# A blocked RWKV inverse spread over all four 64x64 parts of TensorE, with another order on ScalarE, VectorE and GpSimd

## What is computed

```python
x = x + 0.5 * swiglu(rmsnorm(x, g), w_gate, w_up, w_down)       # every ffn stage
# the even stage, for 8 heads of width 64
def step(S, inp):
    Sa = einsum('bhvk,bhk->bhv', S, a_t)
    S = S * w_t + Sa[..., None] * b_t + v_t[..., None] * k_t
    return S, einsum('bhvk,bhk->bhv', S, r_t)
y = concat([y_conv, group_norm(scan(step)) * g]) @ w_out
```

## Time and profile before

| what | us |
|---|---|
| median of 3 runs | 1596.88 |
| lowest and highest of them | 1595.38, 1597.02 |
| the profiled execution, its own time | 1597.77 |
| its span | 1596.0 |
| its TensorE busy | 1543.1 |
| mean granted TensorE clock | 0.991 of full speed |

### The profile page before, as it was taken

How to read it: one execution, slowest core, us unless ns; L and a number is a source line. 1 busy time by engine, 2 the same in 40 slices (tenths; PEclk the granted TensorE clock), 3 DMA queues, 4 the chain that set the end, 5 groups by cost and what they waited for, 6 DMA issues and landing times.

```text
span 1596.0 us, 29271 instructions
## 1 busy us (share of the span) xinstructions
PE 1543.1 (97%) x11720; PEld 1419.5 (89%) x11720; DVE 790.1 (50%) x1053; ACT 766.6 (48%) x1054; POOL 515.2 (32%) x201
## 2 busy tenths in 40 slices
PE   7999999999999999999989999999999999999997
PEld 7999988887999998999976899999999987899996
DVE  4444446467544444434555544345443488754343
ACT  5444364335534453443565544436444478454433
POOL 2443400000444345344342243443434300043442
PEclk9999999999999999999999999999999999999999
DMA  6555431134545535544532355444554452245442
GB/s 254 200 190 197 171 119 68 55 108 158 192 169 192 196 120 198 195 178 178 201 115 74 124 198 192 181 179 163 196 197 183 172 198 93 91 174 197 175 180 92
DMA packets 48086, 259.93 MB, mean 163 GB/s; under 512 B 5376, under 2 KB 5632, under 8 KB 27296
## 3 DMA queue, kind: packets, MB, share of 16 engines
q1 hardware_dynamic: 47664, 258.68, 44.0%
q10 hardware_dynamic: 288, 0.34, 0.1%
q0 software_dynamic: 80, 0.14, 0.0%
HBM read 258.08 MB, written 1.05 MB: 162 GB/s over the span
## 4 chain that ended last, share of the span: by engine, by line
PE 89%; ACT 4%; DVE 4%; issue 1%; DMA 1%; POOL 1%; SPq 0%; DVEq 0%; POOLq 0%; ACTq 0%
PE banks L367 81%; PE banks L1257 1%; ACT gu_hi L338 1%; DVE gu_lo L347 1%; DMA raw_gu<-units_gu 1%; DVE x L474 1%; PE banks L1264 1%; ACT arena L402 1%; PE banks L2048 1%; PE banks L2643 0%; ACT h_hi L385 0%; PE banks L1234 0%; PE banks L2047 0%; DVE arena L2371 0%; ACT arena L2253 0%
## 5 line engine op out<-in xcount | busy, mean ns | idle before, releaser
L360 POOL TENSOR_TENSOR dn_lo<-raw_dn,dn_hi 128x1024 fp32r<-128x1024 f32 x138 | 479.9, 3477 | 905.9 <-ACT dn_hi L343 887.3
L367 PE MATMUL banks<-h_hi,gu_hi 128*128 128x256 f32 x2256 | 644.2, 286 | 11.3 <-DVE h_lo L418 6.7
L367 PE MATMUL banks<-h_hi,gu_lo 128*128 128x256 f32 x2256 | 640.3, 284 | 0.0
L367 PE MATMUL banks<-h_lo,gu_hi 128*128 128x256 f32 x2256 | 640.3, 284 | 0.0
L347 DVE TENSOR_TENSOR gu_lo<-raw_gu,gu_hi 128x2048 fp32r<-128x2048 f32 x161 | 370.2, 2300 | 218.5 <-ACT gu_hi L338 218.3
L367 PEld LDWEIGHTS banks<-h_hi,gu_hi 128*128 128x128 f32 x2256 | 434.5, 193 | 18.5 <-issue 6.1
L367 PEld LDWEIGHTS banks<-h_lo,gu_hi 128*128 128x128 f32 x2256 | 434.5, 193 | 6.1 <-issue 1.4
L367 PEld LDWEIGHTS banks<-h_hi,gu_lo 128*128 128x128 f32 x2256 | 434.2, 192 | 0.0
L338 ACT CAST gu_hi<-raw_gu 128x2048 fp32r<-128x2048 f32 x161 | 306.3, 1903 | 40.1 <-DMA raw_gu<-units_gu 24.8
L482 ACT ACTIVATE silu<-silu 128x256 f32<-128x256 f32 x132 | 55.2, 418 | 520.0 <-DVE silu L490 519.9
L367 PE MATMUL banks<-dn_hi,act_hi 128*128 128x512 f32 x528 | 207.6, 393 | 3.4 <-POOL dn_lo L360 3.4
(11 more groups left out here) (336 smaller groups left out, 1324.3 us busy)
## 6 DMA issues: line engine op xcount, KB each, us to landing
raw_gu<-units_gu SPq DMA_DIRECT2D x161, 1024.0 KB, 5.8
raw_dn<-units_dn SPq DMA_DIRECT2D x162, 512.0 KB, 3.5
x<-x_in SPq DMA_DIRECT2D x2, 512.0 KB, 5.2
raw_gu<-units_gu SPq DMA_DIRECT2D x2, 512.0 KB, 7.5
out<-x SPq DMA_DIRECT2D x1, 1024.0 KB, 3.9
cst<-constants SPq DMA_DIRECT2D x1, 688.0 KB, 12.2
lora<-low_rank SPq DMA_DIRECT2D x1, 512.0 KB, 12.9
arena<-final_gain SPq DMA_DIRECT2D x1, 512.0 KB, 4.1
```

The source lines that it names most:

```text
L360: nc.gpsimd.tensor_tensor(dn_lo[:, p, 0:n], raw_dn[:, p, 0:n], dn_hi[:, p, 0:n].bitcast(F32), ALU.subtract).then_inc(dn_lo_ready, 1)
L367: ins = nc.tensor.matmul(out, a, b, start=first and i == 0, stop=last and i == 2)
```

## The change

1. The steps "x" and `turn_m` go into one function `crossing`. It walks over q, half h of the problems, and c. For h = 0 problem c writes the partitions that it reads, as before; for h = 1 it writes the other half. "inc" stays as it was, since its two inputs are now swapped alike. "g" and "uw" get the same crossing, and the order of "uw" alternates between the two halves.
2. Since MT now holds its second half of problems with the partitions swapped, `scores("ab")` computes the products of g = 1 a second time, crossed, into bank 4, and VectorE reads MT from banks 2 and 4. The turned "a" is made in two steps: `turn_a_crossed` for the heads of partitions 64 to 127 on level 0 (banks 4 and 5), and `turn_a` for the others on level 1. ScalarE copies both.
3. ScalarE splits gu of unit 3 ahead of the exponentials, and gu of unit 5 one level earlier. VectorE takes the rest of unit 3 ahead of "kh", and the rest of unit 5 between the two halves of level 2. `convolution(2)` goes behind `next_state(2)` and `add_y(2)`. The first three `y_conv`, `conv_hi` and `conv_lo` are done ahead of "rstd_y" and of tile 25's end; tile 25 signals after four k-steps for it.
4. In every ffn stage but the first, `hi_dn` of unit 0 stands ahead of the squares of the second half, and the first two units of ScalarE's loop are written out. GpSimd does dn_lo of unit 0 ahead of the "early" part, and dn_lo of unit 1 behind it.

```diff
-        def ffn_act(act, pair, p, f, ahead):
-            hi_dn(act, pair, p)
+        def ffn_act(act, pair, p, f, ahead, split=True):
+            if split:
+                hi_dn(act, pair, p)
...
                 squares_act(act, s, 0)
                 h_hi_act(act, s)
+                hi_dn(act, b, 0)
                 squares_act(act, s, 1)
                 inverse_root_act(act, s)
...
             nc.scalar.preload_act_table(ACT.Silu)
             rstd_row_act(act, s)
-            first = 0
-            if b == 0:
-                ffn_act(act, 0, 0, 0, True)
-                ffn_act(act, 0, 1, 1, True)
-                first = 1
-            with act.Fori(first, HALF - 1) as i:
+            ffn_act(act, b, 0, f, True, s == 0)
+            ffn_act(act, b, 1, f + 1, True)
+            with act.Fori(1, HALF - 1) as i:
                 ffn_act(act, b + i, 0, f + 2 * i, True)
                 ffn_act(act, b + i, 1, f + 2 * i + 1, True)
             i = HALF - 1
...
-        def ffn_all_pool(pool, s):
+        def ffn_all_pool(pool, s, prepare):
             b = first_pair[s]
-            for p in range(2):
-                lo_dn_pool(pool, b, p)
+            lo_dn_pool(pool, b, 0)
+            if prepare is not None:
+                pool.wait_ge(consts_loaded, 32)
+                prepare(pool, s + 1)
+            lo_dn_pool(pool, b, 1)
...
+            def copy_a(g, first):
+                return cp(ga.rearrange("p (g b q) c -> p g b q c", g=2, b=2)[:, g, :, :, CHUNK:P],
+                          two(first)[:, :, 0:256].rearrange("p b (q c) -> p b q c", c=CHUNK))
...
                 if name == "a":
-                    after(act, "dve", "ec")
-                    for b in range(2):
-                        ins = cp(ga.rearrange("p (g b q) c -> p b g q c", g=2, b=2)[:, b, :, :, CHUNK:P],
-                                 banks[:, 6 + b, :].rearrange("p (q g c) -> p g q c", g=2, c=CHUNK))
+                    ins = copy_a(0, 6)
...
             evac(7)
+            hi_gu(act, *unit(s, 3))
             after(act, "pe", "cumsum")
...
             done(ins, "factor")
-            hi_gu(act, *unit(s, 3))
             after(act, "pe", "gate_in")
...
                 if l < NL - 1:
                     copy_m(l, 0)
                     copy_m(l, 1)
+                if l == 0:
+                    after(act, "pe", "a_crossed")
+                    after(act, "dve", "ec")
+                    done(copy_a(1, 4), "a_crossed")
                 evac(11 + l)
                 if l == 0:
                     hi_dn(act, *unit(s, 4))
-                if l == 2:
+                if l == 1:
                     hi_gu(act, *unit(s, 5))
...
+            after(act, "pe", "tile 25 begun")
+            conv_hi(0, 3)
             after(act, "act", "ln_y")
             done(nc.scalar.activation(flat(RSY), flat(RSY), ACT.Exp, scale=-0.5), "rstd_y")
             evac(25)
-            for j in range(4):
-                after(act, "dve", ("y_conv", j))
-                done(cp(h_hi[:, j, :], c4(YC)[:, j, :]), ("conv_hi", j))
+            conv_hi(3, 4)
...
+            def masked(slot, b, mask, name, apart=1):
+                pair = two(b) if apart == 1 else banks[:, b:b + 4, :].rearrange("p (i b) n -> p i b n", b=2)[:, :, 0]
                 done(tt(arena[:, slot, 0:1024].rearrange("p (b q t) -> p b q t", b=2, t=CHUNK),
-                        two(b).rearrange("p b (q t) -> p b q t", t=CHUNK),
+                        pair.rearrange("p b (q t) -> p b q t", t=CHUNK),
...
+                between()
...
+            lo_gu(dve, *unit(s, 3))
             after(dve, "act", "factor")
             done(tt(flat(KH), flat(KC), flat(AI), ALU.mult), "kh")
-            lo_gu(dve, *unit(s, 3))
             mix(8)
...
-            masked(MT, 2, "pairs2", "mt0")
+            masked(MT, 2, "pairs2", "mt0", 2)
...
-            level(2)
-            lo_gu(dve, *unit(s, 5))
+            level(2, lambda: lo_gu(dve, *unit(s, 5)))
             mix(13)
...
             lo_gu(dve, *unit(s, 8))
             convolution(1)
-            convolution(2)
             next_state(2)
             add_y(2)
+            convolution(2)
...
+            for some in ((0, 1, 2), (3,)):
+                for j in some:
+                    after(dve, "act", ("evac", 22 + j))
+                    own(("tap2", j))
+                    done(tt(c4(YC)[:, j, :], c4(CB)[:, j, :], c4(CC)[:, j, :], ALU.mult), ("y_conv", j))
+                for j in some:
+                    after(dve, "act", ("conv_hi", j))
+                    done(tt(h_lo[:, j, :], c4(YC)[:, j, :], h_hi[:, j, :].bitcast(F32), ALU.subtract), ("conv_lo", j))
             lo_dn(dve, *unit(s, 9))
...
                 for j, m, g, c in QUADS:
-                    t = chunk_of(2 * m + c)
-                    ins = mm(banks[rows64(c), b + g, (2 * j + m) * CHUNK:(2 * j + m + 1) * CHUNK], c4(left)[rows64(g), j, t],
+                    t, at = chunk_of(2 * m + c), (2 * j + m) * CHUNK
+                    ins = mm(banks[rows64(c), b + g, at:at + CHUNK], c4(left)[rows64(g), j, t],
                              c4(right)[rows64(g), j, t], start=True, stop=True)
+                    if crossed and g == 1:
+                        ins = mm(banks[rows64(1 - c), b + 2, at:at + CHUNK], c4(left)[rows64(g), j, t],
+                                 c4(right)[rows64(g), j, t], start=True, stop=True)
                 done(ins, name)
...
+            def turn_a():
+
+                for j in range(4):
+                    for m in range(2):
+                        at = (j % 2 * 2 + m) * CHUNK
+                        ins = mm(banks[:, 6 + j // 2, at:at + CHUNK], c4(AT_)[0:64, j, m * P:(m + 1) * P],
+                                 const("eye2")[0:64, :], start=True, stop=True)
+                done(ins, ("tok", "a"))
+
+            def turn_a_crossed():
+
+                for j in range(4):
+                    for m in range(2):
+                        at = (j % 2 * 2 + m) * CHUNK
+                        for c in range(2):
+                            ins = mm(banks[rows64(1 - c), 4 + j // 2, at:at + CHUNK], c4(AT_)[64:P, j, chunk_of(2 * m + c)],
+                                     const("eye2")[64:P, :], start=True, stop=True)
+                done(ins, "a_crossed")
...
+            def crossing(name, bank, left, right):
+
                 for q in range(8):
-                    for c in range(2):
-                        ins = mm(banks[rows64(c), 6 + h, q * CHUNK:(q + 1) * CHUNK], prob(MT)[rows64(c), 8 * h + q, :],
-                                 const("eye2")[rows64(c), :], start=True, stop=True)
-                done(ins, ("m", l, h))
+                    for h in range(2):
+                        for c in range(2):
+                            ins = mm(banks[rows64(1 - c if h else c), bank + h, q * CHUNK:(q + 1) * CHUNK],
+                                     prob(left)[rows64(c), 8 * h + q, :],
+                                     const("eye2")[rows64(c), :] if right is None else prob(right)[rows64(c), 8 * h + q, :],
+                                     start=True, stop=True)
+                        if q == 7:
+                            done(ins, (*name, h))
...
+            scores("ab", BT_, AT_, 2, crossed=True)
             tile(9)
             after(pe, "dve", "mt1")
             after(pe, "act", "gate")
-            turn_m(-1, 0)
-            turn_m(-1, 1)
+            turn_m(-1)
...
-                for h in range(2):
-                    after(pe, "act", ("m", l - 1, h))
-                    by_problem(("x", l, h), h, 2, AB, MI)
+                after(pe, "act", ("m", l - 1, 1))
+                crossing(("x", l), 2, AB, MI)
                 if l == 2:
                     after(pe, "dve", "kt")
-                if l < 3:
+                if l == 1:
+                    after(pe, "act", "a_crossed")
+                    turn_a()
+                elif l < 3:
                     turn(TOKS[l], c4(tok_source[TOKS[l]]))
...
                 tile(11 + l, range(2, 5))
                 if l < NL - 1:
                     after(pe, *(("act", ("tok", TOKS[l])) if l < 3 else ("dve", "ak")))
-                    for h in range(2):
-                        after(pe, "dve", ("mt", l, h))
-                        turn_m(l, h)
+                    after(pe, "dve", ("mt", l, 1))
+                    turn_m(l)
+                    if l == 0:
+                        turn_a_crossed()
                 tile(11 + l, range(5, KD))
...
                     for g in range(2):
                         for c in range(2):
-                            ins = mm(banks[rows64(c), 4 + g, (2 * j + m) * CHUNK:(2 * j + m + 1) * CHUNK],
+                            ins = mm(banks[rows64(1 - c if g else c), 4 + g, (2 * j + m) * CHUNK:(2 * j + m + 1) * CHUNK],
...
-            for q in range(16):
+            for q in (q + 8 * g for q in range(8) for g in range(2)):
                 for c in range(2):
```

(56 more changed lines are left out.)

6 lines of the change are left out of this document (3 added, 3 removed).

## The result

| | before | after |
|---|---|---|
| median, us (5 runs each, taken together) | 1596.88 | 1587.36 |
| lowest and highest | 1592.64, 1598.78 | 1586.09, 1588.18 |
| ratio, 95% interval | | 0.9942 (0.9930 to 0.9953) |
| the profiled execution, its span | 1597.77, 1596.0 | 1588.18, 1586.4 |
| mean granted TensorE clock | 0.991 | 0.990 |

The change makes the kernel 9.5 us faster. I forecast 1578.5 and a range up to 1584.0, so the direction was right and the size was not: about half of the gain is missing. The first line of the page answers to the earlier trace rows; TensorE's busy time has fallen by 10.7 us, GpSimd's and VectorE's have grown.

What follows compares the result with a forecast made beforehand. TensorE, busy 97% of the span, was taken as the bound. Terms -11.8 + 2.6 - 5.0 - 1.8 + 1.2 - 0.3 - 1.3 + 1.05 - 3.0 = -18.4 us gave 1578.5 us after run-median adjustment; range 1574.5 to 1584.

Steps and rivals of the forecast that it cites:

- Part 1: Even stage's crossed steps: 11 steps at 1.09 instead of 2.01 us, "uw" 1.7 less; together 11.8 us less.
- (b): Crossed steps: four parts do not run at once when both row halves write both banks; 1590.3 us, chance 0.06.
- (c): Crossed steps run one product after the other, twice today's time; slower, 1618 us, chance 0.02.
- Part 2: Swapped layout's cost in the even stage: "ab" 0.9, turn_a_crossed 1.0, turn_a 1.7, less one turn; 2.6 us more.
- Part 3: Even stage's moved splits: gap and slow clock 5.0 us less, "inc" wait 1.8, y_state 0.3, row start 1.3 less.
- The new waits in the levels: Even stage: less TensorE time to hide other engines; 0.5 on level 0, 0.5 on level 4, 1.2 us more altogether.
- (a): Even stage's covers fail, levels bound by VectorE and ScalarE, 0.8 per level instead of 0.25; 1583 us, chance 0.12.
- (d): Early split of unit 3 does nothing and the clock still falls; 5.0 back, 1583.5 us, chance 0.04.
- Part 4: Ffn stages with early hi_dn: 1.05 us more in the third stage, 3.0 less in the fourth.
- The third stage's 1.05: hi_dn ahead of ScalarE's chain, for which TensorE already waits at the third stage's start: 1.05 us more.
- The whole 3.0: Fourth stage: the 3.4 us wait for unit 0's dn_lo goes, 0.4 given back at unit 1; 3.0 us less.
- each dn_lo between 2.4 and 4.5: Fourth stage on GpSimd: spread of dn_lo's duration in us, by which unit 1 would give back 0 to 1.7.

Runs made afterwards that it cites:

- even_only: The changed kernel without part 4 (ffn stages and GpSimd as before): 1579.96 us, ratio 0.9893 to before.
- ffn_only: The kernel before with part 4 alone: 1604.83 us, ratio 1.0043 to before.
- best2: split_prepare with three of unit 4's and unit 5's splits moved earlier in the even stage: 1577.06 us, ratio 0.9878 to before.
- split_prepare: even_only with GpSimd doing dn_lo of unit 0 amid the mla preparation, unit 1's behind it: 1576.08 us, ratio 0.9861 to before.
- prepare_late: even_only with GpSimd's mla and fox preparations behind dn_lo of both first units: 1583.42 us, ratio 0.9904 to before.
- wait_diag: The changed kernel, but GpSimd's dn_lo of unit 0 waits for VectorE's diagonals in all stages but the first: 1584.71 us, ratio 0.9921 to before.
- act_rstd: The changed kernel with rstd_half and both diagonals made on ScalarE instead of VectorE: 1581.90 us, ratio 0.9895 to before.

## Why the prediction was right and wrong

**Part 1, the crossed steps: right.** 1.09 to 1.11 us a step against 1.09 forecast, "uw" 1.91 against 1.9. Rivals (b) and (c) are out: both row halves write both banks, and four parts run at once. The rule that I quoted against my own sum (different row tiles cannot use the same bank at the same time) costs nothing in any of these steps: they take the 1.09 us that `scores` takes with a bank for each row half.

**Part 2: right, a little cheap.** "ab" takes 2.02 against 2.0, `turn_a` 1.93 against 1.7. `turn_a_crossed` takes 0.22 + 0.97 = 1.19 against 1.0, but 1.09 us of "issue" stand in its middle, with no semaphore in the profile that TensorE waits for.

**Part 3: right where it was simplest.** The gap of 3.4 us and the slow stretch behind it are gone, and so are the wait ahead of "inc" and those at `y_state` and the row start. The wait moved to "mean" (1.4 us), as forecast. The new waits in the levels are two ahead of "inc", on levels 0 and 4 where I had put them, 0.7 in all against 1.2. The 0.6 at L1304 is not one of them: before waits as long there, at its `turn_m` and for the same mask:

```profile
PE banks L1264 <- DVE arena L983: 0.7, 1, 0.7
```

Two terms that I did not have nearly cancel: a slow stretch of before at 204.9 us is gone (1.6), another came at 234.8 (1.5 more). Together with parts 1 and 2 I had -16.4; the stage is 16.1 us shorter, and `even_only` is 17.2 us faster. Rivals (a) and (d) do not explain the miss: the levels held their covers but for 0.7 us, and unit 3's early split did its work.

**Part 4: this is the step that failed.** Forecast +1.05 - 3.0 = -2.0 us; measured +7.7 (`ffn_only`). Of the 7.7 the waits account for 5.4 to 5.9 (4.0 to 4.2 at L448, 0.9 to 1.0 for gu_lo, 0.4 to 0.8 for dn_lo); for the rest no cause is shown. Term by term:

- The third stage's 1.05 was right: TensorE's gap there is 1.3 instead of 0.4.
- "In the others gu of unit 1 is split before, VectorE makes the inverse root's row behind its gu_lo, and 1.05 is covered." This is wrong. I counted ScalarE's 1.05 and not what `hi_dn` sets off: GpSimd's dn_lo, which had been waiting for it, now starts ahead of `rstd_half` and stops VectorE until it ends. Four stages lose about 1 us each at L448 (after less `even_only`: 5.2 - 1.2 = 4.0).
- "So dn_lo of unit 0 starts at about 589.2 and the 3.4 us go." The start was exact: 574.53 in after is 589.2 in the time of before, as everything is 14.7 us earlier. What followed was not. dn_lo took 4.5 and not 3.5, and the preparation behind it 16.4 and not 12.2, because its DMA now travels behind weight loads and one more of its small operations meets a gu_lo. I had unit 1's dn_lo start at 604.9; it started at 595.50 + 14.7 = 610.2. The 5.3 us between them are these two terms, 1.0 and 4.2. TensorE, itself held 1.0 at L448, waits 3.5 us for it. The whole 3.0 that I took off was paid back, at unit 1 instead of unit 0.

So the rival that decided was not among mine. My "each dn_lo between 2.4 and 4.5" used the very rows that show the lock, as a spread. The commonest pair of instructions in the kernel shows it. VectorE in before, at 617 us, and GpSimd beside it:

```profile
617.22 2.29 DVE L347 TENSOR_TENSOR gu_lo<-raw_gu,gu_hi 128x2048 fp32r<-128x2048 f32 x1 [0.98 <-ACT gu_hi L338]
```

```profile
618.21 3.56 POOL L360 TENSOR_TENSOR dn_lo<-raw_dn,dn_hi 128x1024 fp32r<-128x1024 f32 x1 [2.25 <-ACT dn_hi L343]
```

gu_lo holds until 619.5; from there to dn_lo's end at 621.8 it is 2.3 us, what dn_lo needs alone. An engine's instruction that takes 2.4, 3.56 or 4.5 us for the same tile is one that waits inside its busy time (nine of after's 138 dn_lo take 2.3 to 2.4, all others 3.5 or more), and the question for each move is what it will now overlap.

**What stays open.** The 1.09 us of "issue" in `turn_a_crossed` is not new work. In before 0.82 us of the same kind stand at 338.76, in the middle of tile 19, and all kernels with `turn_a_crossed` have 1.1 to 1.5 ahead of its eighth instruction and nothing in tile 19. There is one such stall of over 0.8 us in the even stage of each kernel, and its place moves with the code. The DMA view has one thing beside it. In after, over 263.50 to 266.10 us (packets, MB, share of the DMA engines):

```profile
q8 instruction: 1, 0.02, 2.2%
```

A load of 16 KB of instructions starts there at 263.85 and takes 0.92 us; TensorE stops at 264.99 and goes on at 266.07. In all eleven kernels such a load starts 0.85 to 1.4 us ahead of the stall, and TensorE goes on 2.2 to 2.4 us after the load's start. So TensorE probably waits for its instructions. That is not shown: I have not tried to move it, and the other loads of this kind in the even stage, about twenty, have no stall of this size behind them. The scatter of the clock is open too, below.

## What to carry to other kernels

An operation that is moved earlier also moves everything that was waiting for it. Before counting such a move as covered, list which engines start sooner and what runs on VectorE and GpSimd at that moment, since these two can stop each other even over 128x2 numbers. When the same instruction on the same shape has two or three different durations in a trace, find out what it overlaps before using any of them as a price.

## What the runs showed of the hardware

**Which of VectorE's operations are stopped.** The list of one line each (min/median/max ns) in after:

```profile
L491 DVE TENSOR_TENSOR silu<-banks,arena x132: 409/424/425, 22.1 to 1571.5; 128x256 f32<-128x256 f32 x132
L493 DVE TENSOR_TENSOR act<-silu,banks x132: 420/421/422, 23.4 to 1572.4; 128x256 f32<-128x256 f32 x132
L496 DVE TENSOR_TENSOR act_lo<-act,act_hi x132: 424/424/1811, 24.3 to 1573.3; 128x256 fp32r<-128x256 f32 x132
L360 POOL TENSOR_TENSOR dn_lo<-raw_dn,dn_hi x138: 2340/3562/4518, 23.1 to 1567.0; 128x1024 fp32r<-128x1024 f32 x138
```

The three operations of VectorE have the same shape and stand close together. The two that take one input from TensorE's banks vary by 16 ns at most in 132 times, though 18 and 14 of them begin while a dn_lo is running. The one with both inputs in the common memory takes up to 1.81 us where it overlaps a dn_lo (10 times), and 0.43 at most elsewhere. `rstd_half`, with one small input and output there, is stopped as well. The same page of the Trainium skill, section "Who interferes with whom", has both: two inputs from that memory make an operation of VectorE contend with those of GpSimd that read it, and tensor_scalar, the kind of `rstd_half`, can contend in its two-port modes. The durations agree; in which mode `rstd_half` ran, no trace here shows.

**The clock.** The slow stretch behind the 3.4 us gap went with the gap, but another came. The chain in after, and a 2 us window in it (busy time of each engine, then the granted clock):

```profile
235.55 4.25 PE banks L367 x24
```

```profile
236.00:238.00 2.00, 2.00 (x12) 2.00 (x11) 0.00 (x0) 1.98 (x5) 0.00 (x0) 0.50 0.00 0
```

The 24 products of this tile took 3.06 in before. TensorE is at 0.50 of full speed, its 1.2 GHz level, though it had been busy without a gap since 209.30. On the other hand the stretch of before at 204.9 is gone. With the one at the program's end, such stretches number between three (`best2`) and eight (before) in these traces; after has seven. That scatter is some microseconds: the executions of `best2` alone lie 10 apart, 1573.03 at a mean granted clock of 0.996 and 1583.06 at 0.989. So the 1.6 us that I counted for the clock in part 3 can be seen at its place, but the total does not show it. What brought the stretch at 234.8 is open.

**The small DMA.** The positions land 2.6 to 2.7 us after issue when no load of weights is issued beside them (in before and `split_prepare` the last one is within 1.1 us of its landing), and 5.1 to 5.8 when two are issued within the next 1.1 us, in `prepare_late`, after, `wait_diag`, `act_rstd` and `ffn_only`. No packet of the small DMA takes more than about 0.2 us in before and `split_prepare`; in after one takes 0.86. What a transfer costs depends on where it is put.
